# Rotary turn of queries and keys by four row transfers instead of a permutation product

## The chip, the cores and the metric

The kernel runs on one core of a Trainium2 chip. The metric is the device time of one execution in microseconds, lower is better. TensorE is PE in the profile (its weight loads are PEld), VectorE is DVE, ScalarE is ACT, GpSimd is POOL, and SP is the engine whose queue fetches the weights.

## The reference, cut to what matters

Two transformer-like blocks are computed for 256 positions of 2048 values. The first has two layers. In each layer a projection `w_in` (2048 to 6144) gives the input of a state-space mixer, gates, and the queries, keys and values of eight heads of differential attention. The change touches only the rotary turn of those queries and keys:

```python
def apply_rope(t, cos, sin):
    half = HEAD_DIM // 2
    tf = t.astype(jnp.float32)
    t1, t2 = tf[..., :half], tf[..., half:]
    return jnp.concatenate([t1 * cos - t2 * sin, t2 * cos + t1 * sin], axis=-1).astype(t.dtype)

q = apply_rope(q.reshape(bsz, s, ATTN_HEADS, 2, HEAD_DIM), cos, sin)
k = apply_rope(k.reshape(bsz, s, ATTN_HEADS, 2, HEAD_DIM), cos, sin)
```

HEAD_DIM is 64, so within each group of 64 rows the two groups of 32 rows change places, and one of them changes its sign. The second block has an RWKV mixer, a latent attention with a small rotary part of its own (tiles `kpe` and `qp`), and a feed-forward part. All arithmetic is float32 within the tolerance of the reference.

## The kernel before, in words

Everything is kept transposed: a tile is 128 features (partitions) by 256 positions. A projection is a stream of output tiles. Each output tile of `w_in` is the sum of 16 blocks, and each block is three matmuls of rounded float32 values (high weight part with high and low activations, low weight part with high activations). The weights are fetched in halves of 8 blocks (512 KB) on SP's queue; ACT makes the high part of a half (`hi`), DVE the low part (`lo`). Four halves of room (`NS = 4`) are kept, so ACT may make half p as soon as PE has finished half p - 4, and there are three halves between the two.

One list of beats, made by the class `Timeline`, fixes the order of work of all five engines. Each engine plays the beats that concern it in that order, with semaphore waits on what the others do. The list is the matmul blocks of the streams; at the end of an output tile its evacuation `ev` begins, phase 0 with the end of the tile, and one further phase at every eighth block after it. In between, background generators give one step each at every second block (`per=2`; every fourth with `per=4`): the state-space mixer (`s5`, 16 rounds per layer, each a preparation `s5_prep` and a run `s5_run`), the attention of a head (`att`, 15 steps) and, in the second block, the RWKV heads (`rw`, 15 steps each, eight heads, in the stream of `w_in2` from tile 28 on). How many background steps lie behind each step of a generator is written out by hand in the tuples `S5_PREP`, `S5_RUN`, `S5_PHASE`, `S5_START`, `ATTENTION`, `RWKV` and `MOD_REST` (the "rests"). In layer 0 a fourth generator, `modulation`, runs matmuls of the 1 MB units of `w_ada`, which share the weight ring.

The tiles of kind `rope` are the query and the key tile of each head: 2 x 8 heads x 2 layers = 32. Their three phases before the change:

- phase 0, ACT (line 1806): wait for the tile's last matmul, copy it from the accumulator to one of four slots in `TMP`.
- phase 1, PE (line 1112): wait for this copy, multiply it with the signed permutation `rot` (float32, 128 x 128 by 128 x 256) into the second half of the same bank.
- phase 2, DVE (line 2457 on): `o` = turned tile x `SIN`, slot = slot x `COS`, `o` = `o` + slot, `o` being the place of the head's query in `QT` or of its key in `KB`. The attention of the head waits for the last of them (semaphore `ropes`).

A bank of the accumulator is handed on after the first of the three operations of DVE (`BANK_FREE`). `RS` and `RS2` are two rows of 256 columns that hold norm sums and roots at other times. ACT's own queue issues four DMAs, all at the start of the kernel (`begin`).

Of the kernel before, what the change touches and what calls it, by code (L numbers as in the profile page):

```python
# [15 lines left out]
MUL, ADD, SUB, MAX, MIN = ALU.mult, ALU.add, ALU.subtract, ALU.max, ALU.min  # L16
# [31 lines left out]
def const_array():  # L48
    p = np.arange(128)
# [3 lines left out]
    def put(name, a):  # L53
        n = dict(CONSTS)[name]
        c[:, CCOL[name]:CCOL[name] + n] = np.asarray(a, np.float32).reshape(128, -1) if np.ndim(a) else a
# [2 lines left out]
    rot = np.zeros((128, 128))  # L58
    for m in range(128):
        if m % 64 < 32:  # L60
            rot[m + 32, m] = -1
        else:
            rot[m - 32, m] = 1
    put("rot", rot)
# [11 lines left out]
    put("scm", np.broadcast_to(np.arange(256) % 32 != 0, (128, 256)))  # L76
    put("id64", p[:, None] % 64 == np.arange(64)[None, :])
    put("ch4", p[:, None] // 32 == np.arange(4)[None, :])
    put("invf", np.float32(10000.0) ** (-(p % 32).astype(np.float32) / np.float32(32)))
    top = p < 64  # L80
    put("sgn", np.where(top, 1, -1))
    put("ph1", np.where(top, 0.25, 0))
# [43 lines left out]
SIN = _c.alloc(256)  # L126
# [62 lines left out]
class Mem:  # L189
# [26 lines left out]
    def V(self, off, *dims, p0=0, np_=128):  # L216
        t, n, o = (self.ar, N1, off) if off < N1 else (self.up, N2, off - N1)
        return bass.AP(tensor=t, offset=p0 * n + o, ap=[[n, np_]] + self.steps(dims))
# [5 lines left out]
    def B(self, bank, off, *dims, p0=0, np_=128):  # L224
        return bass.AP(tensor=self.ps, offset=p0 * 4096 + bank * 512 + off, ap=[[4096, np_]] + self.steps(dims))
# [22 lines left out]
    def PT(self, k):  # L248
# [8 lines left out]
          "qn": 1, "qp": 3, "kn": 1, "v2": 3, "brw": 1, "bmla": 3, "mo": 2, "up0": 4, "up1": 5, "e": 1, "d0": 1,  # L257
          "d1": 3, "pg": 4}

BANK_FREE = {"u": "ev_act", "z": "ev_dve", "rope": "ev_dve", "v": "ev_act2", "ga": "ev_act", "gb": "ev_act",  # L260
             "xa": "ev_dve", "xo": "ev_dve", "xf": "ev_dve", "rw": "ev_rs", "kpe": "ev_dve", "cq": "ev_rs", "gate": "ev_rs", "qn": "ev_act",
             "qp": "ev_dve", "kn": "ev_act", "v2": "ev_act2", "brw": "ev_dve", "bmla": "ev_dve", "mo": "ev_act",
             "up0": "ev_rs", "up1": "ev_rs", "e": "ev_act", "d0": "ev_act", "d1": "ev_dve", "pg": "ev_act"}
# [11 lines left out]
def kind_of(name, n):  # L275
# [19 lines left out]

QUADS = (("w_in", 48), ("w_pg", 0))

S5_PREP = ((0, 0, 3, 7, 1, 5, 0, 3, 0),
    (0, 2, 0, 4, 2, 6, 2, 2, 0))
S5_RUN = ((1, 3, 1, 7, 1, 3, 1, 2),  # L300
    (1, 5, 2, 6, 1, 3, 1, 1))
S5_PHASE = ((18, 1),
    (17, 2))
S5_START = (6, 8)
ATTENTION = ((1, 1, 3, 2, 3, 4, 4, 1, 2, 1, 1, 2, 5, 2, 1),
    (1, 1, 2, 2, 1, 1, 4, 1, 5, 2, 3, 3, 3, 1, 2))
RWKV = (1, 3, 3, 6, 3, 4, 2, 2, 2, 1, 2, 2, 2, 4, 1)
MOD_REST = (2, 3, 2)


class Tile:
# [634 lines left out]
class Port:  # L946
# [22 lines left out]
    def put(self, ins):  # L969
        self.newest = Op(self, ins)  # L970
        return self.newest
# [118 lines left out]
def tensor_program(pe, m, tl, D):  # L1090
# [18 lines left out]

    def ev(t, ph):  # L1110
        b = t.bank
        if t.kind in ("rope", "qp", "kpe") and ph == 1:
            pe.wait_ge("ev_rs" if t.kind == "kpe" else "ev_act", ("ev", t.o))
            pe.mm(B(b, 256, 256), con("rot"), V(TMP + 256 * t.slots[0][0], 256), True, True).then_inc("ev_pe", ("ev", t.o))
        if t.kind in ("v", "v2") and ph == 1:
            s = TMP + 256 * t.slots[0][0]
            pe.wait_ge("ev_act", ("ev", t.o))
            pe.tr(B(b, 256, 128), V(s, 128))
            pe.tr(B(b, 384, 128), V(s + 128, 128)).then_inc("ev_pe", ("ev", t.o))
# [391 lines left out]
def scalar_program(act, m, tl, D):  # L1511
# [280 lines left out]
    def ev(t, ph):  # L1792
# [13 lines left out]
        elif t.kind in ("rope", "v", "qp", "v2") and ph == 0:  # L1806
            s = tile_ready(act, t.slots[0])
            act.act(V(s, 256), pv, ACT.Copy).then_inc("ev_act", key)
        elif t.kind in ("v", "v2") and ph == 2:
            hd = (n - 8) // 4  # L1810
            if t.kind == "v" and hd >= 2:
# [95 lines left out]
def vector_program(dve, m, tl, D):  # L1907
# [535 lines left out]
    def ev(t, ph):  # L2443
# [10 lines left out]
        if t.kind == "z" and ph == 1:  # L2454
            dve.wait_ge("ev_act", key)
            dve.stt(s, s, 1.0, pv, ADD, MUL).then_inc("ev_dve", key)
        elif t.kind in ("rope", "qp", "kpe") and ph == 2:
            if t.kind == "rope":
                hd = (n - 8) // 4
                o = V(KB + 256 * (hd % 2) if (n - 8) % 4 else QT + 256 * hd, 256)  # L2460
# [2 lines left out]
            else:  # L2463
                o = V(KPE if t.kind == "kpe" else QP + 256 * (n - 8), 256)
            dve.wait_ge("table_act", 1 if t.kind == "rope" else 2)
            dve.wait_ge("ev_pe", key)
            dve.tt(o, B(b, 256, 256), V(SIN, 256), MUL).then_inc("ev_dve", key)
            dve.tt(s, s, V(COS, 256), MUL)
            dve.settle()
            dve.tt(o, o, s, ADD).then_inc("ropes", key)  # L2470
# [460 lines left out]
```

## Time and profile before

| what | us |
|---|---|
| three runs | 2893.70, 2898.98, 2899.66 |
| median | 2898.98 |
| the profiled execution | 2895.5 |
| its span, first to last instruction | 2893.6 |
| PE busy | 2781.8 (96%) |
| DVE busy | 2008.9 (69%) |
| ACT busy | 1468.2 (51%) |
| DMA share of the 16 engines | 54.2% for SP's queue, 5.4% for POOL's |

The granted TensorE clock is 0.985 of 2.4 GHz over the span. Times of stretches are counted from the first instruction. Matched with the list of beats, the stretches are: layer 0's `w_in` from tile 8 on about 168 to 524, the rest of layer 0 to 698, layer 1's `w_in` from tile 8 on about 750 to 1045 (its rope tiles end at 984), RWKV heads 1354 to 1698, the tail of RWKV to 1739. A busy PE is no measure of speed, since matmuls overlap; the start-to-start time of the big matmuls is.

### The profile page before, as it was taken

What the parts mean: (1) busy time and instruction counts of PE and PEld (TensorE: products, weight loads), DVE (VectorE), ACT (ScalarE), POOL (GpSimd) and SP (SyncE); (2) the same over time, 40 slices, a digit from 0 to 9 for tenths busy, and PEclk for the clock granted to TensorE, in tenths of its full rate; (3) what the DMA queues carried; (4) which work ended last, traced back from release to release, by engine and by line L of the source; (5) the groups of instructions that cost most, each with busy time, mean ns of one, the idle gap of its engine ahead of it and who ended that gap; (6) DMA issues with size and microseconds to landing.
All of it is one profiled execution on the core that took longest, in us unless ns stands there. A gap on an engine that the chain in (4) does not pass through costs nothing.

```text
span 2893.6 us, 64415 instructions
## 1 busy us (share of the span) xinstructions
PE 2781.8 (96%) x27664; PEld 2593.9 (90%) x27664; DVE 2008.9 (69%) x3478; ACT 1468.2 (51%) x2406; POOL 288.5 (10%) x488
## 2 busy tenths in 40 slices
PE   6899999999999999999999999999999999999987
PEld 2678788788999999999889889999999999999987
DVE  6357778687799986765556566666888547887565
ACT  3335556355566656644444435456555445555454
POOL 0012222100123221200011011100000000000000
PEclk9899999999999999999999999999999999999999
DMA  9988788885756566555444445554555555555543
GB/s 392 332 267 269 260 287 267 292 310 169 205 171 199 175 204 197 181 175 169 140 144 150 140 133 170 180 193 161 185 182 187 184 184 180 181 185 187 182 153 110
DMA packets 168236, 581.08 MB, mean 201 GB/s; under 512 B 40272, under 2 KB 40304, under 8 KB 155536
## 3 DMA queue, kind: packets, MB, share of 16 engines
q1 hardware_dynamic: 146784, 525.40, 54.2%
q0 software_dynamic: 20592, 48.26, 5.4%
q8 instruction: 218, 3.57, 0.5%
q10 hardware_dynamic: 576, 3.31, 0.3%
q14 instruction: 66, 0.54, 0.1%
HBM read 555.06 MB, written 21.76 MB: 199 GB/s over the span
## 4 chain that ended last, share of the span: by engine, by line
PE 84%; DVE 7%; DMA 6%; ACT 1%; issue 1%; SPq 1%; POOL 0%; DVEq 0%; ACTq 0%
PE acc L1011 82%; DMA arena<-in_w_ada 3%; DVE arena L979 2%; PE acc L1014 2%; DVE rounded L979 2%; DMA scr_k<-arena 1%; DMA arena<-scr_k 1%; SPq L976 1%; DVE upper L987 1%; DMA scr_u<-upper 0%; DVE arena L987 0%; ACT arena L1008 0%; DVE rounded L987 0%; DVE upper L979 0%; DMA arena<-in_w_outm 0%
## 5 line engine op out<-in xcount | busy, mean ns | idle before, releaser
L1011 PE MATMUL acc<-rounded 128*128 128x256 f32 x14592 | 1861.9, 286 | 18.6 <-issue 10.1
L1011 PEld LDWEIGHTS acc<-rounded 128*128 128x128 f32 x14592 | 1783.5, 192 | 86.2 <-issue 61.2
L1008 ACT ACTIVATE rounded<-arena 128x1024 fp32r<-128x1024 f32 (+1 forms) x862 | 875.3, 1022 | 694.5 <-PE acc L1011 583.5
L979 DVE TENSOR_TENSOR rounded<-arena,rounded 128x1024 fp32r<-128x1024 f32 (+1 forms) x830 | 983.9, 1198 | 246.7 <-ACT rounded L1008 246.1
L1011 PEld LDWEIGHTS acc<-upper_rounded,rounded 128*128 128x128 f32 x4656 | 560.8, 192 | 18.2 <-issue 9.8
L1011 PE MATMUL acc<-upper_rounded,rounded 128*128 128x256 f32 x4656 | 567.7, 284 | 2.8 <-DVE rounded L979 2.0
L1008 ACT ACTIVATE arena<-arena 128x256 f32<-128x256 f32 (+3 forms) x473 | 232.9, 515 | 170.8 <-DVE arena L979 105.4
L979 DVE TENSOR_TENSOR arena<-acc,arena 128x256 f32<-128x256 f32 (+5 forms) x270 | 113.7, 431 | 233.7 <-PE acc L1011 221.0
L979 DVE TENSOR_TENSOR arena<-arena 128x256 f32<-128x256 f32 (+5 forms) x455 | 233.3, 526 | 35.9 <-ACT arena L1008 27.5
L987 DVE SCALAR_TENSOR_TENSOR arena<-arena 128x256 f32<-128x256 f32 (+5 forms) x465 | 205.1, 446 | 27.7 <-ACT arena L1008 19.6
L1011 PE MATMUL acc<-arena 128*32 128x512 f32 (+6 forms) x1990 | 183.2, 402 | 41.7 <-DMA arena<-in_w_ada 27.6
L1008 ACT ACTIVATE arena<-acc 128x256 f32<-128x256 f32 (+3 forms) x267 | 99.2, 384 | 187.6 <-PE acc L1011 179.2
L1011 PEld LDWEIGHTS acc<-arena 128*32 128x32 f32 (+2 forms) x1990 | 69.6, 123 | 97.0 <-DMA arena<-in_w_ada 50.7
L1008 ACT ACTIVATE upper<-acc 128x128 f32<-128x128 f32 (+3 forms) x184 | 67.4, 380 | 114.2 <-PE acc L1011 82.5
L1008 ACT ACTIVATE arena<-acc,arena 128x256 f32<-128x256 f32 (+1 forms) x148 | 59.3, 428 | 103.3 <-PE acc L1011 91.2
L1011 PE MATMUL acc<-upper 32*32 32x32 f32 (+8 forms) x4384 | 101.3, 218 | 9.1 <-issue 3.3
L1011 PEld LDWEIGHTS acc<-upper 32*32 32x32 f32 (+4 forms) x4384 | 73.1, 114 | 30.0 <-issue 13.5
L976 POOL DMA_DIRECT2D arena<-scr_k x128 | 77.3, 621 | 122.5 <-DMA scr_k<-arena 121.8
L1011 PE MATMUL acc<-upper,arena 64*64 64x64 f32 (+4 forms) x490 | 63.0, 350 | 13.7 <-DMA upper<-in_w_ada 6.9
L976 POOL DMA_DIRECT2D scr_g<-arena x56 | 30.4, 545 | 440.4 <-DVE arena L990 236.6
L1014 PE MATMUL acc<-arena 128*128 128x128 f32 x416 | 71.2, 276 | 2.8 <-ACT arena L1008 2.3
L1008 ACT ACT_TABLE_LOAD x56 | 71.8, 1283 | 4.0 <-issue 3.0
(92 smaller groups left out, 1116.0 us busy)
## 6 DMA issues: line engine op xcount, KB each, us to landing
arena<-in_w_in SPq DMA_DIRECT2D x328, 512.0 KB, 4.8
arena<-in_w_ada SPq DMA_DIRECT2D x88, 1024.0 KB, 5.5
arena<-in_w_up SPq DMA_DIRECT2D x176, 512.0 KB, 3.9
arena<-in_w_down SPq DMA_DIRECT2D x88, 512.0 KB, 4.2
arena<-in_w_outa SPq DMA_DIRECT2D x32, 512.0 KB, 6.0
arena<-in_w_glu SPq DMA_DIRECT2D x32, 512.0 KB, 5.8
arena<-in_w_outm SPq DMA_DIRECT2D x32, 512.0 KB, 4.6
arena<-in_w_out SPq DMA_DIRECT2D x32, 512.0 KB, 3.8
```

The source lines that it names most:

```text
L976: self.e.dma_start(out, in_).then_inc(self.signals.sems[sem], 16)
L979: return self.put(self.e and self.e.tensor_tensor(o, a, b, op))
L987: return self.put(self.e and self.e.scalar_tensor_tensor(out=o, in0=a, scalar=s, in1=b, op0=o1, op1=o2))
L1008: return self.put(self.e and self.e.activation(o, a, f, scale=scale, **kw))
L1011: return self.put(self.e and self.e.matmul(o, l, r, start=start, stop=stop, skip_group_check=True))
L1014: return self.put(self.e and self.e.transpose(o, i, self.m.con("ident")))
```

## The change

1. The PE instruction of phase 1 is gone for `rope` tiles. `kpe` and `qp` tiles keep it.
2. ACT, after its copy of phase 0, waits until DVE has done with the tile that used the same row four tiles earlier (from tile 12 on), waits for its own copy, and issues four DMAs on its own queue. Each moves 32 rows of 256 values (32 KB) of the slot to the neighbouring group of 32 rows of `RS` (query tiles) or `RS2` (key tiles).
3. DVE's first operation of phase 2 waits for these four DMAs instead of PE, and reads `RS` or `RS2` instead of the accumulator.
4. The sign is moved from `rot` to the table of frequencies, so that `SIN` comes out signed; `COS` is even and stays.
5. The bank is free after ACT's copy.
6. The rests are different.

```diff
-            rot[m + 32, m] = -1
+            rot[m + 32, m] = 1
...
-    put("invf", np.float32(10000.0) ** (-(p % 32).astype(np.float32) / np.float32(32)))
+    put("invf", np.where(p % 64 < 32, -1, 1) * np.float32(10000.0) ** (-(p % 32).astype(np.float32) / np.float32(32)))
...
-BANK_FREE = {"u": "ev_act", "z": "ev_dve", "rope": "ev_dve", "v": "ev_act2", "ga": "ev_act", "gb": "ev_act",
+BANK_FREE = {"u": "ev_act", "z": "ev_dve", "rope": "ev_act", "v": "ev_act2", "ga": "ev_act", "gb": "ev_act",
...
-S5_PREP = ((0, 0, 3, 7, 1, 5, 0, 3, 0),
-    (0, 2, 0, 4, 2, 6, 2, 2, 0))
-S5_RUN = ((1, 3, 1, 7, 1, 3, 1, 2),
+S5_PREP = ((0, 0, 3, 7, 2, 5, 0, 2, 1),
+    (0, 2, 3, 3, 0, 6, 2, 2, 0))
+S5_RUN = ((1, 4, 1, 7, 1, 3, 1, 1),
     (1, 5, 2, 6, 1, 3, 1, 1))
-S5_PHASE = ((18, 1),
-    (17, 2))
-S5_START = (6, 8)
-ATTENTION = ((1, 1, 3, 2, 3, 4, 4, 1, 2, 1, 1, 2, 5, 2, 1),
-    (1, 1, 2, 2, 1, 1, 4, 1, 5, 2, 3, 3, 3, 1, 2))
-RWKV = (1, 3, 3, 6, 3, 4, 2, 2, 2, 1, 2, 2, 2, 4, 1)
-MOD_REST = (2, 3, 2)
+S5_PHASE = ((13, 6),
+    (18, 1))
+S5_START = (5, 8)
+ATTENTION = ((1, 1, 3, 2, 3, 4, 4, 1, 1, 1, 1, 2, 6, 2, 1),
+    (1, 1, 2, 2, 1, 1, 4, 1, 5, 1, 3, 4, 3, 1, 2))
+RWKV = (2, 4, 4, 5, 3, 1, 1, 1, 1, 1, 2, 3, 3, 3, 1)
+MOD_REST = (2, 3, 1)
...
-        if t.kind in ("rope", "qp", "kpe") and ph == 1:
+        if t.kind in ("qp", "kpe") and ph == 1:
...
             act.act(V(s, 256), pv, ACT.Copy).then_inc("ev_act", key)
+            if t.kind == "rope":
+                if n >= 12:
+                    act.wait_ge("ev_dve", ("ev", tl.out_of["w_in", l, n - 4].o))
+                act.wait_ge("ev_act", key)
+                for q in range(4):
+                    act.dma(V((RS, RS2)[n % 4], 256, p0=32 * q, np_=32), V(s, 256, p0=32 * (q ^ 1), np_=32), f"swap{n % 4}", (t.o, q))
...
-            dve.wait_ge("ev_pe", key)
-            dve.tt(o, B(b, 256, 256), V(SIN, 256), MUL).then_inc("ev_dve", key)
+            if t.kind == "rope":
+                dve.wait_ge(f"swap{n % 4}", (t.o, 3))
+                half = V((RS, RS2)[n % 4], 256)
+            else:
+                dve.wait_ge("ev_pe", key)
+                half = B(b, 256, 256)
+            dve.tt(o, half, V(SIN, 256), MUL).then_inc("ev_dve", key)
```

## Rows read from the trace of the kernel before

**Rows 1.** Busy time by stretch; the columns are named in the second line.

```profile
core 0: us, PE busy (x) PEld busy (x) DVE busy (x) ACT busy (x) POOL busy (x), PEclk, DMA share, GB/s
200.00:524.00 324.00, 319.28 (x2838) 263.38 (x2837) 256.41 (x482) 180.18 (x378) 77.33 (x129) 1.00 0.81 271
750.00:984.00 234.00, 232.03 (x2146) 218.43 (x2145) 212.21 (x397) 146.75 (x308) 65.86 (x108) 1.00 0.60 183
1354.00:1698.00 344.00, 332.50 (x6927) 303.98 (x6926) 194.01 (x394) 149.01 (x266) 32.57 (x60) 1.00 0.44 143
1698.00:1739.00 41.00, 36.89 (x612) 34.33 (x611) 27.69 (x51) 11.06 (x16) 7.34 (x11) 0.96 0.35 114
```

**Rows 2.** The chain that ended last, shares of the span by engine.

```profile
PE 84%; DVE 7%; DMA 6%; ACT 1%; issue 1%; SPq 1%; POOL 0%; DVEq 0%; ACTq 0%
```

**Rows 3.** Timeline of PE, layer 1: start, us, instruction, shapes, count.

```profile
753.19 6.00 PE L1011 MATMUL acc<-rounded 128*128 128x256 f32 x48
759.12 0.64 PE L1011 MATMUL acc<-arena,upper 128*32 128x128 f32 x16
...
766.02 1.70 PE L1011 MATMUL acc<-rounded 128*128 128x256 f32 x12
767.56 0.59 PE L1011 MATMUL acc<-arena 128*128 128x256 f32 x2
767.80 3.23 PE L1011 MATMUL acc<-rounded 128*128 128x256 f32 x24
770.87 0.82 PE L1014 MATMUL acc<-arena 128*128 128x128 f32 x6
```

**Rows 4.** Timeline of ACT's queue at the start: its only four DMA issues.

```profile
0.72 0.41 ACTq L976 DMA_DIRECT2D arena<-in_params  x1
...
2.12 0.77 ACTq L976 DMA_DIRECT2D arena<-in_x  x1
```

**Rows 5.** The line of all DMA issues, and issues by tensor (KB, us to landing).

```profile
L976 SPq DMA_DIRECT2D arena<-in_w_in x328: 327/328/1931, 90.5 to 1673.1; - x164
DMA to landing us min/median/max: 2.0/4.4/20.5
...
arena<-scr_k POOLq DMA_DIRECT2D x128, 64.0 KB, 4.8
arena<-in_params ACTq DMA_DIRECT2D x1, 8.0 KB, 5.2
```

**Rows 6.** Timelines of ACT and DVE: three rope tiles, copy and first operation.

```profile
917.25 0.36 ACT L1008 ACTIVATE arena<-acc 128x256 f32<-128x256 f32 x1
917.52 1.05 ACT L1008 ACTIVATE rounded<-arena 128x1024 fp32r<-128x1024 f32 x1
...
920.48 0.42 DVE L979 TENSOR_TENSOR upper<-acc,arena 128x256 f32<-128x256 f32 x1
...
757.07 0.39 ACT L1008 ACTIVATE arena<-acc 128x256 f32<-128x256 f32 x1 [1.27 <-PE acc L1011]
...
761.37 0.42 DVE L979 TENSOR_TENSOR upper<-acc,arena 128x256 f32<-128x256 f32 x1 [1.70 <-PE acc L1011]
...
442.26 0.36 ACT L1008 ACTIVATE arena<-acc 128x256 f32<-128x256 f32 x1
...
453.26 0.42 DVE L979 TENSOR_TENSOR upper<-acc,arena 128x256 f32<-128x256 f32 x1
```

**Rows 7.** Who PE waited for, 200 to 524.

```profile
PE acc L1011 <- DMA arena<-scr_k: 2.6, 2, 1.9
```

**Rows 8.** Timeline of ACT and PE inside RWKV head 3, steps 8 and 9.

```profile
1515.16 0.28 ACT L1008 ACTIVATE upper<-acc 128x128 f32<-128x128 f32 x1 [0.31 <-PE acc L1011]
...
1516.65 0.45 PE L1011 MATMUL acc<-upper 32*32 32x32 f32 x32
```

**Rows 9.** Timeline of PE at the end of RWKV, after the last block of `w_in2`.

```profile
1732.86 4.33 PE L1011 MATMUL acc<-arena,upper 128*64 128x128 f32 x48 [0.77 <-DVE upper L993]
1738.01 1.09 PE L1011 MATMUL acc<-arena,upper 128*64 128x128 f32 x16 [0.83 <-DVE arena L979]
```

More of the change, by code:

```diff
@@ L2456, in ev @@
             dve.stt(s, s, 1.0, pv, ADD, MUL).then_inc("ev_dve", key)
-        elif t.kind in ("rope", "qp", "kpe") and ph == 2:
+        elif t.kind in ("qp", "kpe") and ph == 2 or t.kind == "rope" and ph == 2:
             if t.kind == "rope":
```

## The prediction

> **What bounds the kernel now.** I read four views in this order. The chain that ended last comes first: PE holds 84% of it, DVE 7%, DMA 6% and ACT 1% [rows 2]. Whatever takes matmul time off PE therefore shortens the kernel, as long as no other engine is close behind. The busy times by stretch say who is close behind [rows 1]. In layer 0 (200 to 524) PE is busy 319.3 of 324 us, DVE 256.4, ACT 180.2. In layer 1 (750 to 984) PE is busy 232.0 of 234 us, but DVE 212.2 as well; only 21.8 us of that stretch is free on DVE. ACT has 146.7 of 234. So layer 0 is PE's alone, while in layer 1 DVE stands some 9% behind PE. Then the timeline of PE gives the price of one permutation product, and the timelines of ACT and DVE side by side give the time that a transfer may take. The clock is 1.00 of 2.4 GHz in both stretches, so it has nothing to give.
>
> **The product that goes.** The cost of a product is the PE time that it inserts between big matmuls. Without anything between them 48 big matmuls take 759.12 - 753.19 = 5.93 us, 0.1235 us each. From 766.02 to 770.87 there are 36 big ones and one product: 4.85 us, less 36 x 0.1235 = 4.45, leaves 0.40 us [rows 3]. The same arithmetic one product earlier, over 24 big ones, gives 0.45. I take 0.42. There are 32 of them, 16 in each layer: 32 x 0.42 = 13.4 us, between 12.8 and 14.4. The product's second record (0.59 us for the pair) overlaps the next matmuls, so 32 x 0.59 would count too much. The weight load goes with it.
>
> **What ACT gets.** Four DMA issues for each rope tile. ACT's queue issued four DMAs in the whole kernel before, in 0.41 to 0.77 us each [rows 4]; on SP one issue takes 0.33 us [rows 5]. I take 0.45, with 0.33 and 0.77 as bounds: 1.8 us for a tile (1.3 to 3.1), 58 us in all (42 to 99). In layer 1 that makes 146.7 + 16 x 1.8 = 175.5 of 234 us, so ACT doesn't become the bound. Queued behind it is nearly always the high part of a weight half: `hi` starts 0.27 us after the copy began [rows 6]. By the code it has until three halves later, 3 x 24 x 0.1235 = 8.9 us, so a delay of 1.8 us does not reach PE that way. It reaches DVE, which makes the low part from it and takes other beats only in order. The wait for the tile four back is over long before (four tiles are 24 us and more), and the wait for its own copy ends with it. I count this part at 0 for PE in layer 0 and put it in the DVE term for layer 1. Without the cover it would be 1.8 us a tile.
>
> **When the swapped rows arrive.** No row shows a transfer from SBUF to SBUF, so I bound it. From issue to landing all DMAs take 2.0 us at least and 4.4 in the median; the smallest one on ACT's queue took 5.2, and the nearest in size, 64 KB, 4.8 [rows 5]. The last of four issues starts 3 x 0.45 = 1.35 us after the copy. Thus the rows are there 1.35 + 4.4 = 5.7 us after the copy, with bounds 3 x 0.33 + 2.0 = 3.0 and 3 x 0.77 + 5.2 = 7.5. DVE's first operation began 2.87 us after the copy's end in the tightest tile (920.48 against 917.61), 3.9 us in another one, where it waited for the product itself, and 10.6 us in one of the loosest [rows 6]. The three stand for 32 tiles; read in the same way for all, the median is 6.9 us, 7 of the 32 are under 5.2 and 12 under 5.9. Adding up what is missing to 5.7 us gives about 4 us of DVE waiting in layer 0 and 7 in layer 1; missing to 3.0 it is 0.1 in all, missing to 7.5 about 15 and 21. The three DVE operations themselves keep their size: 0.42 us from the accumulator, 0.41 from SBUF [rows 6]. In layer 0 DVE has 68 us free [rows 1] and the wait is hidden.
>
> **A rule that speaks against it.** The trace has transfers to landing in 2.0 to 5.2 us at these sizes [rows 5]. The Trainium skill, "DMA: Bandwidth & Descriptors", section "Rules for kernel authors", says that transfers under 64 KB pay mostly overhead, and that transfers to disjoint partition groups serialize, so one for all partitions is better. If the four came one after another by the page's fixed 2 us, the rows would be there about 8 us after the copy, an estimate from that page. Rows can't decide it, and it is the slower rival below, priced from rows.
>
> **What it comes to in layer 1.** PE would need 6.7 us less there, so DVE's 21.8 us of free time shrink to 15.1. Of these, from the count of DVE's operations, some 5 us are gaps under 0.2 us between dependent operations that don't compress. The remaining 10 must hold the 7 us of waiting for rows and whatever ACT's delay adds (16 tiles at up to 1.8 us, mostly hidden by beats in between; I take 3). That is just enough; PE begins to feel single late low parts. I take 2 us lost, between 0 and 7 (the whole gain of this layer).
>
> **The bank** that is free earlier brings nothing: it is used again three tiles later, after DVE's operation in every tile I looked at, and PE names no wait for it. The signed table costs no instruction.
>
> **The rests.** RWKV: the tuple sums to 38 steps before and 35 after, of two blocks each. Eight heads end 8 x 3 x 2 = 48 blocks earlier, 48 x 3 x 0.1235 = 17.8 us of matmuls, so the closing steps that now run alone after the last block fall into the stream. PE's free time in that tail is 41 - 36.9 = 4.1 us, two pieces of it 0.77 and 0.83 [rows 1, 9]; the rest of it is PE work that stays. I take 2 us gained, 0 to 4. Against it, the rests behind steps 5 to 8 fall to 1, that is by 0.74 us a step in three of four. PE came 1.21 us after ACT's copy in such a step (1516.65 against 1515.44) [rows 8], so 0.47 us is left; a `hi` of 1.05 us in front of that copy would turn it into a stall. I take 1.5 us lost, 0 to 8. In layer 0 the run's step 4 moves one step away from the load of the taps, for which PE waited 2.6 us [rows 7]: 1.5 us gained, 0 to 3. The other rests shift single steps by 0.7 us and sum to the same; 0, plus or minus 2. `MOD_REST` moves eight units earlier by one step each, once 0.9 us at most. Sum of the rests: -2, from -9 to +12.
>
> **Sum.** -13.4 + 2 - 2 = -13.4 us. Against the profiled execution, 2895.5 us, that is 2882; the median of the three runs is 3.5 us above it, and against this median it is 2885.6. I predict 2886.
>
> **Rivals.**
> 1. The rows come late and DVE becomes the bound in layer 1. Point from which it decides: rows later than about 7 us after the copy. At 9.5 us, four landings behind each other at 2.0 to 2.4 us, 14 of 16 tiles wait and the missing time sums to about 45 us; less the 10 us of compressible free time and less the lead of the low parts, about 5 us once, PE loses 30 us and gains 6.7, while layer 0 still gains 6.7 and hides its 36 us. Net +16, 2915. For it: the only ACT issue of a small transfer took 5.2 us. Against: that one flew beside 2 MB of others, and the DMA share is 0.60 in layer 1.
> 2. The gain is real in layer 0 only. ACT's 1.8 us and the rows' waits together take up DVE's free time: 6.7 us of layer 1 gone, the shortened RWKV rests cost 3 more instead of bringing anything: -13.4 + 6.7 + 1 = -5.7, 2893. For it: DVE at 212 of 234.
> 3. The rests are worth more than I can count from sums: stalls in front of the mixer's steps and in RWKV go as well, 8 us more: 2877.
> 4. The change doesn't shorten PE, because the stream is paced by weight fetches. In layer 0 the DMA share is 0.81 [rows 1]. Then 2899. Against: PE names 2.6 us of DMA waits in 324 us [rows 7].
>
> **How the numbers follow.** Forecast (2879 to 2892) 0.57; rival 3 (under 2879) 0.11; rival 2 (2892 to 2900) 0.15; rival 4 (2896 to 2902) 0.04; rival 1 (over 2902) 0.13. A measurement of this kernel can tell about 0.2%, 5.8 us, so faster means under 2893.2. It has the forecast, rival 3 and a quarter of rival 2: 0.72. Slower means over 2904.8: rival 1 but for its mild end, 0.12. Same: 0.16. The range leaves out most of rival 1 and the end of rival 3: 2874 to 2904.
>
> **What would show it.** Right: no product records in the stretches of `w_in`; the stretch from 200 to 984 shorter by some 12 us; the first DVE operation of a rope tile named as waiting for the transfer in about a third of tiles, up to 3 us. Wrong: issues on ACT above 0.8 us; landing after more than 7 us; DVE free time near nothing in layer 1 with PE waiting for `rounded` from DVE; more than 5 us of new PE waits between 1354 and 1698. The forecast also fails if the new rests cost something in the mixer's rounds that their sums don't show.

## The result, and the profile after

The changed kernel takes 2916.94 us (median of 6 runs, 2912.99 to 2927.02), the kernel before 2898.27. The ratio is 1.0066, with a 95% interval from 1.0048 to 1.0084: slower by 19 us, where 2886 was forecast. The profiled execution of after spans 2914.5 us.

The rows of after that answer to [rows 1] are these (the same stretches of time, which hold less work once the kernel is behind; the columns are the same). PE's busy time falls by 3.3 us in layer 0 and by 14 us in layer 1. Neither is a saving: in layer 0 PE is idle for 8.1 of 324 us, where it was for 4.7, and in layer 1 for 16 of 234 us, where it was for 2.

```profile
200.00:524.00 324.00, 315.94 (x2799) 261.45 (x2799) 256.92 (x482) 180.04 (x376) 75.69 (x129) 0.99 0.83 278
750.00:984.00 234.00, 217.97 (x1983) 203.62 (x1982) 200.28 (x372) 136.50 (x289) 62.19 (x101) 0.99 0.58 180
```

The chain that ended last, shares by engine (before: [rows 2]). PE has lost 5 points of it; ACT, ACT's queue and "issue" have gained 5 together, DVE one.

```profile
PE 79%; DVE 8%; DMA 6%; ACT 3%; issue 2%; ACTq 2%; SPq 0%; POOL 0%; DVEq 0%
```

The new issues, from the line of all DMA issues of after (duration of one in ns: least, median, most; before: [rows 4, 5]):

```profile
L976 ACTq DMA_DIRECT2D arena<-arena x128: 513/613/1750, 178.6 to 989.2; - x128
```

Their row in the list of issues by tensor (KB, median us to landing):

```profile
arena<-arena ACTq DMA_DIRECT2D x128, 32.0 KB, 4.1
```

One issue takes 0.61 us in the median and up to 1.75, against the 0.45 that I took. A single transfer lands as quickly as I took it, 4.1 us after its issue. All four of a tile are there 6.4 us after the copy's end in the median and 9.3 us at most, where I had 5.7 with 7.5 as the upper bound.

To see where the 19 us come from I cut the kernel into stages, at PE's first product of a stage's output tile. Three stages matter: `w_in` of layer 0 and of layer 1, each from tile 8, where the rope tiles are, and RWKV's part, from the first block that carries it to the first product of `q_up`. The table has all runs of this study. "Nothing" is the time in RWKV's part for which PE stood and the profile names no releaser ("issue" in the rows). The ratio is that of the whole kernel to runs of before made beside it (their medians lie from 2896.7 to 2899.7 us), with its interval.

| run | layer 0 | layer 1 | RWKV | "nothing" | median us, ratio |
|---|---|---|---|---|---|
| before | 355.7 | 295.3 | 386.9 | 4.4 | 2898.27 |
| e11_before_again | 355.3 | 295.3 | 392.6 | 6.4 | one run |
| after | 354.8 | 311.8 | 394.3 | 9.5 | 2916.94, 1.0066 (1.0048 to 1.0084) |
| e1_old_rests | 358.0 | 308.7 | 397.0 | 11.0 | 2925.53, 1.0088 (1.0075 to 1.0102) |
| e3_no_swap | 350.2 | 293.5 | 396.6 | 9.9 | 2899.57, 0.9996 (0.9986 to 1.0006) |
| e12_no_swap_again | 351.1 | 293.3 | 399.0 | 9.0 | one run |
| e4_issue_no_wait | 362.3 | 304.3 | 394.5 | 9.7 | 2923.51, 1.0085 (1.0071 to 1.0099) |
| e10_two_issues | 356.0 | 296.6 | 392.4 | 5.9 | 2905.74, 1.0027 (1.0013 to 1.0041) |
| e5_sp_issue | 356.1 | 300.3 | 395.5 | 8.1 | 2909.0, 1.0037 (1.0024 to 1.0050) |
| e9_pool_issue | 353.9 | 305.4 | 393.7 | 8.6 | 2912.35, 1.0048 (1.0032 to 1.0064) |
| e7_dummy_product | 347.7 | 294.0 | 389.4 | 4.9 | 2894.45, 0.9985 (0.9976 to 0.9995) |
| e2_new_rests | 351.2 | 296.1 | 406.5 | 15.8 | 2908.52, 1.0039 (1.0023 to 1.0054) |
| e6_rwkv_rests | 351.7 | 295.3 | 411.4 | 21.1 | 2911.58, 1.0047 (1.0033 to 1.0061) |
| e8_early_rests | 355.2 | 296.0 | 396.6 | 6.9 | 2898.35, 0.9999 (0.9987 to 1.0012) |
| e13_pad_half | 349.9 | 295.4 | 394.4 | 8.2 | 2901.12, 1.0011 (1.0001 to 1.0020) |
| e16_pad_full | 354.1 | 295.3 | 393.7 | 6.3 | 2897.41, 1.0003 (0.9990 to 1.0016) |
| e14_new_rests_pad | 353.0 | 296.1 | 397.2 | 11.3 | 2905.55, 1.0020 (1.0007 to 1.0032) |
| e15_rwkv_rests_pad | 352.3 | 295.3 | 396.9 | 12.4 | 2902.49, 1.0016 (1.0007 to 1.0026) |

Before it is read, one thing about its grain. Layer 1 repeats to 0.2 us from one profile to the next. RWKV's part doesn't: before itself shows 386.9 and 392.6, and e8, whose instructions there are the same, 396.6. Layer 0 lies between 349.9 and 355.7 in kernels with the same mechanism there. So layer 1 can be read to a few tenths, the other two only by several profiles or by the ratios.

The same stage in whole, before and after, then who PE waited for in it (us in total, times, longest) and whom DVE waited for most:

```profile
750.00:1045.40 295.40, 292.66 (x2711) 276.40 (x2710) 270.05 (x504) 187.23 (x389) 83.48 (x137) 1.00 0.59 183
```

```profile
747.20:1059.00 311.80, 292.65 (x2678) 274.17 (x2677) 271.32 (x505) 186.81 (x389) 82.62 (x137) 0.99 0.57 180
```

PE's waits there, before:

```profile
PE acc L1011 <- DVE upper L979: 1.5, 2, 1.0
PE acc L1014 <- ACT arena L1008: 0.8, 1, 0.8
```

and after:

```profile
PE acc L1014 <- ACT arena L1008: 8.1, 10, 1.8
PE acc L1014 <- DVE arena L987: 5.6, 4, 3.1
PE acc L1011 <- ACT upper L1008: 2.4, 2, 1.9
```

DVE's waits in the same stage, after:

```profile
DVE rounded L979 <- ACT rounded L1008: 18.6, 13, 4.5
DVE upper L979 <- DMA arena<-arena: 4.1, 4, 2.7
```

The wait for the new rows themselves is small (4.1 us, on DVE, and 5.2 in layer 0). What has grown are waits for ACT: PE's from 0.8 to 8.1 us, and DVE's for `rounded` from 3.9 to 18.6. In layer 0 the same line of PE's waits grows from 1.5 us,

```profile
PE acc L1014 <- ACT arena L1008: 1.5, 1, 1.5
```

to 7.2:

```profile
PE acc L1014 <- ACT arena L1008: 7.2, 6, 1.8
```

One place shows how. The timeline of ACT, PE and DVE of after:

```profile
828.45 0.36 ACT L1008 ACTIVATE arena<-acc 128x256 f32<-128x256 f32 x1
...
828.89 3.58 ACTq L976 DMA_DIRECT2D arena<-arena  x4
...
832.52 1.06 ACT L1008 ACTIVATE rounded<-arena 128x1024 fp32r<-128x1024 f32 x1 [3.71 <-issue]
833.48 0.36 ACT L1008 ACTIVATE arena<-acc 128x256 f32<-128x256 f32 x1
833.61 1.23 DVE L979 TENSOR_TENSOR rounded<-arena,rounded 128x1024 fp32r<-128x1024 f32 x1 [0.55 <-ACT rounded L1008]
...
833.90 0.44 PE L1014 MATMUL acc<-arena 128*128 128x128 f32 x2 [1.82 <-ACT arena L1008]
```

The rope tile is copied at 828.45. ACT then issues four transfers, for 3.58 us, and runs nothing meanwhile. Behind them stand a `hi` and, behind that, a copy of the mixer's run (`xt`, out of the accumulator). PE makes its two transposes from this copy, and stands still 1.82 us for it. By the shapes and the number of transposes, 5.8 of the 8.1 us of such waits in layer 1 are for copies of the mixer, the rest for copies of the attention.

### The profile page after: what moved, and what is told of

The parts are those of the page before. It is cut to its first block, busy times and chain, and to the rows that moved or that the text cites. A ratio compares the mean times of both kernels' runs of the same rounds, so it can differ in the third digit from the quotient of the medians.

```text
span 2914.5 us, 64420 instructions
## 1 busy us (share of the span) xinstructions
PE 2780.6 (95%) x27600; PEld 2591.2 (89%) x27600; DVE 2009.3 (69%) x3478; ACT 1467.0 (50%) x2406; POOL 286.7 (10%) x488
## 4 chain that ended last, share of the span: by engine, by line
PE 79%; DVE 8%; DMA 6%; ACT 3%; issue 2%; ACTq 2%; SPq 0%; POOL 0%; DVEq 0%
PE acc L1011 78%; DMA arena<-in_w_ada 3%; DVE arena L979 3%; DVE rounded L979 2%; ACTq L976 2%; ACT arena L1008 1%; PE acc L1014 1%; ACT rounded L1008 1%; DMA upper<-in_w_ada 1%; DVE arena L987 1%; DVE upper L987 1%; ACT L1008 1%; DVE upper L979 0%; DVE rounded L987 0%; DMA scr_k<-arena 0%
## 5 line engine op out<-in xcount | busy, mean ns | idle before, releaser
L1011 PE MATMUL acc<-arena 128*32 128x512 f32 (+7 forms) x1926 | 166.6, 404 | 37.9 <-DMA arena<-in_w_ada 24.5
L1011 PEld LDWEIGHTS acc<-arena 128*32 128x32 f32 (+2 forms) x1926 | 61.5, 122 | 88.8 <-DMA arena<-in_w_ada 46.0
L1014 PEld LDWEIGHTS acc<-arena 128*128 128x128 f32 x416 | 48.1, 141 | 30.2 <-ACT arena L1008 19.1
```

What stands on the lines that cost most here:

```text
L1011: return self.put(self.e and self.e.matmul(o, l, r, start=start, stop=stop, skip_group_check=True))
L1014: return self.put(self.e and self.e.transpose(o, i, self.m.con("ident")))
```

## Experiments

The theory after the comparison: ACT's four issues delay its own copies, and that is the loss. The rival: DVE waits for the rows' landing. A second question is why RWKV's part is longer, in which the mechanism changes nothing.

The runs e3, e4, e5, e7, e9, e10 and e12 are made from the changed kernel with before's rests; its signed table and its earlier bank stay.

**e1_old_rests.** The change with the tuples of rests of before: the mechanism alone.

```
-RWKV = (2, 4, 4, 5, 3, 1, 1, 1, 1, 1, 2, 3, 3, 3, 1)
+RWKV = (1, 3, 3, 6, 3, 4, 2, 2, 2, 1, 2, 2, 2, 4, 1)
...   and S5_PREP, S5_RUN, S5_PHASE, S5_START, ATTENTION, MOD_REST likewise
```

> The changed kernel with all rests of the kernel before. Theory A: the four issues on ACT (0.61 us each in the changed kernel, 2.5 us a tile) hold up the small ACT steps of the mixer and of the attention that PE waits for, and the new rests cost only in RWKV, where PE took 394.2 us instead of 386.8. Then this one gives some 2909, with layer 1's w_in from tile 8 on near 310 us and RWKV near 387. Theory B: the loss is all in the new rests, the transfers do what they should. Then 2885, with layer 1 near 289.

Measured: 2925.53 us, ratio 1.0088, above both expectations. The mechanism alone costs 25 us. Layer 1 is at 308.7 us, where theory A had it, but RWKV's part takes 397.0 us with the old rests too, so the new rests are not what lengthens it. They give 6 us back (1.0088 to 1.0066), which is about the uncertainty of that difference.

**e2_new_rests.** Before with the new tuples, that is with those lines the other way round: the rests alone.

> The kernel before with the new rests alone, the product stays on PE. Theory A: RWKV 7 us longer, the rest within 3: 2905. Theory B: all of the loss plus the missing gain: 2917 + 13 = 2930, with layer 1 above 310 us.

Measured: 2908.52 us, 1.0039. With the product in place the same rests cost 11 us. What they bring seems to be no fixed amount; e6 and e8 take this up.

**e3_no_swap.** No product and no transfer: DVE multiplies the slot itself by the sines (the turned half of the rope is left out).

```
-        if t.kind in ("rope", "qp", "kpe") and ph == 1:
+        if t.kind in ("qp", "kpe") and ph == 1:
...
-            dve.wait_ge("ev_pe", key)      # for rope tiles alone
-            dve.tt(o, B(b, 256, 256), V(SIN, 256), MUL)
+            dve.wait_ge("ev_act", key)
+            dve.tt(o, s, V(SIN, 256), MUL)
```

> Old rests, no product and no transfers: DVE multiplies the slot itself by the sines, so the turned half is left out of the computation. This is what the change could gain at most: 32 x 0.42 = 13.4 us, 2885. If DVE is the bound of layer 1, as the prediction feared, the 6.7 us of that layer come out smaller than those of layer 0: 2890 or more.

Measured: 2899.57 us, 0.9996. Without any cost of the swap, taking the products away brings nothing that can be told. Layer 1 shows why, first the stage in whole:

```profile
745.00:1038.50 293.50, 286.71 (x2679) 271.09 (x2677) 270.06 (x503) 186.83 (x389) 83.94 (x137) 1.00 0.60 183
```

and whom PE waited for in it:

```profile
PE acc L1014 <- DVE arena L987: 2.3, 4, 1.0
PE acc L1011 <- DVE upper L979: 2.0, 2, 1.0
PE acc L1014 <- ACT arena L1008: 1.9, 3, 0.8
```

PE is busy 286.7 us instead of 292.7, 6 us less, 0.37 a product. But the stage is only 1.9 us shorter: PE's free time has grown from 2.7 to 6.8 us, in front of operations of DVE and ACT, which are as busy as before (270.1 and 186.8). In layer 0 PE's busy time falls by 6.9 us. The stage is shorter by some 3.5: the three profiles without the old product or a transfer (e3, e12, e7) have 349.7 us in the mean, the six with the product and the same early rests (before, e11, e6, e13, e15, e16) 353.2, and the two groups overlap. And RWKV's part is 4 to 12 us longer than in the two profiles of before, with not one instruction changed in it. So the total of this run is a small gain and a loss elsewhere that has nothing to do with the swap.

**e4_issue_no_wait.** e3, and ACT issues four transfers of the same size for each rope tile, out of the table of cosines; the results are not used, and DVE waits only once in a layer, at the last step of attention, for the last of them (the turned half is left out).

```
+            if t.kind == "rope":
+                act.wait_ge("table_act", 1)
+                if n >= 12:
+                    act.wait_ge(f"swap{n % 4}", (tl.out_of["w_in", l, n - 4].o, 3))
+                act.wait_ge("ev_act", key)
+                for q in range(4):
+                    act.dma(V((RS, RS2)[n % 4], 256, p0=32 * q, np_=32),
+                            V(COS, 256, p0=32 * (q ^ 1), np_=32), f"swap{n % 4}", (t.o, q))
...
+            if h == 7:              # DVE, attention, step 14
+                for part in range(2):
+                    dve.wait_ge(f"swap{part}", (tl.out_of["w_in", l, 36 + part].o, 3))
```

> As e3_no_swap, and ACT issues its four transfers (from the cosine table into the rows, so the turned half is left out of the computation), but nobody waits for their landing at once. Theory A, the issues cost: the same as e1_old_rests within 3 us. Theory C, the landing costs (DVE waits and the low parts come late): near e3_no_swap, 2885 to 2890.

Measured: 2923.51 us, 1.0085; e3 has 0.9996 beside the same runs of before. Issuing alone costs 26 us (12 in layer 0 and 11 in layer 1 by the table), and with the wait for the landing (e1) the ratio is 1.0088. So the landing adds 1 us, give or take 6, and the rival falls as the main cause. PE's waits in layer 1, without any landing to wait for:

```profile
PE acc L1014 <- ACT arena L1008: 6.8, 10, 1.3
PE acc L1014 <- DVE arena L987: 5.0, 4, 2.6
PE acc L1011 <- ACT upper L1008: 2.2, 2, 1.8
```

These are nearly the waits of after; in layer 0 the wait for ACT's copies is 12.8 us.

**e10_two_issues.** e4 with two issues.

```
-                for q in range(4):
+                for q in range(2):
```

> As the run in which ACT issues four transfers that nobody waits for, with two issues a tile instead of four (the turned half of the rope stays left out). If each issue delays ACT's next copies by its own length and PE feels all of it: layer 1's w_in about 299 us, half way between 293.5 (none) and 304.3 (four), and 2911 us in all. If there is slack to be used up first: 295 us and 2902 in all.

Measured: 2905.74 us, 1.0027, between the two expectations. Layer 1 takes 293.5, 296.6 and 304.3 us with none, two and four issues: the first two cost 3 us there, the second two 8. Two issues (1.14 us, at 572 ns each) mostly fit into what the copies of layer 1 had in hand; the next two don't. In layer 0 the steps are more alike (350.2 or 351.1, 356.0 and 362.3 us). The whole kernel loses 9 us with the first two and 17 with the second. PE's waits, the same lines:

```profile
PE acc L1014 <- ACT arena L1008: 2.9, 4, 1.3
PE acc L1014 <- DVE arena L987: 2.5, 3, 1.3
```

**e5_sp_issue.** e1, with the issues on SP's queue.

```
+    def ev(t, ph):          # in sync_program; the same lines are gone from scalar_program
+        if t.kind == "rope" and ph == 0:
+            n, l, s = t.n, t.l, TMP + 256 * t.slots[0][0]
+            if n >= 12:
+                sp.wait_ge("ev_dve", ("ev", tl.out_of["w_in", l, n - 4].o))
+            sp.wait_ge("ev_act", ("ev", t.o))
+            for q in range(4):
+                sp.dma(...)
```

> The changed kernel with the rests of before, its four row transfers issued by SP instead of ACT; everything else, the wait of DVE for the landing included, stays. Theory (what costs is that ACT's own copies queue behind four issues of 0.6 us): layer 1's w_in (mm 1152 to 1920) back to about 351 us as in the run without transfers, from 364 to 368, and 2900 us in all (2896 to 2904). Rival (the rows come too late, DVE waits): 2920 or more, since the landing is the same or later on SP's queue, which also issues the weights. The stretch of RWKV should be 381 us as in the other runs without products, whoever issues.

Measured: 2909.0 us, 1.0037, between what the two expected. Moving the issues off ACT takes away 15 of the 25 us, most of it, not all. The same transfers still fly, so it is not their traffic that costs: PE's waits for ACT's copies in layer 1, 10.4 us in e1, are 2.4 us. What shows in layer 1 now is that DVE waits for the rows. DVE's longest waits there:

```profile
DVE upper L979 <- DMA arena<-arena: 9.2, 2, 5.9
```

and PE's:

```profile
PE acc L1014 <- DVE arena L987: 4.7, 3, 3.6
PE acc L1011 <- DVE upper L979: 3.4, 3, 1.4
```

Two waits only, but one of 5.9 us. The transfers themselves land sooner than on ACT's queue (3.2 us after issue in the median). It is the issue that comes late, as the timeline of this wait shows:

```profile
755.97 5.24 SPq L976 DMA_DIRECT2D upper<-scr_u  x6
756.45 0.38 ACT L1008 ACTIVATE arena<-acc 128x256 f32<-128x256 f32 x1 [1.27 <-PE acc L1011]
...
761.26 2.41 SPq L976 DMA_DIRECT2D arena<-arena  x4
...
764.95 0.42 DVE L979 TENSOR_TENSOR upper<-arena 128x256 f32<-128x256 f32 x1 [5.91 <-DMA arena<-arena]
```

The copy ends at 756.83. SP is in the middle of six other issues and comes to these four at 761.26, 4.4 us later. In most tiles it comes within 0.1 us.

**e9_pool_issue.** The same on POOL's queue.

```
+        elif t.kind == "rope" and ph == 0:     # in gpsimd_program
+            if n >= 12:
+                pool.wait_ge("ev_dve", ("ev", tl.out_of["w_in", l, n - 4].o))
+            pool.wait_ge("ev_act", key)
+            for q in range(4):
+                pool.dma(...)
```

> The changed kernel with the rests of before, its four row transfers issued by POOL instead of ACT. POOL has little work beside w_in, but its issues may take longer and wait for its own stores. Theory (issues cost only what is queued behind them): layer 1's w_in as with SP or better, 296 to 301 us of 308.7 with ACT, and about 2905 us in all (2899 to 2910). Rival (the last 9 us that SP's version keeps above the run without transfers are the landing, which DVE waits for): no better than SP's, 2909 or more.

Measured: 2912.35 us, 1.0048. An issue takes 0.51 us there, but DVE waits 12.7 us in layer 1 for the rows (5 times, 4.6 at most), and the stage takes 305.4 us. POOL's program waits in order for the landing of other transfers (123 us in 31 waits for `scr_k` in the whole run), and its first issue comes 0.3 us after the copy in the median but 8.5 us in the worst tile. The rival of this run holds: no queue of the three carries the swap for free.

**e6_rwkv_rests and e8_early_rests.** Before with RWKV's new tuple alone (the line below), and with all the other new tuples but that one.

```
-RWKV = (1, 3, 3, 6, 3, 4, 2, 2, 2, 1, 2, 2, 2, 4, 1)
+RWKV = (2, 4, 4, 5, 3, 1, 1, 1, 1, 1, 2, 3, 3, 3, 1)
```

> Before with only the tuple of RWKV's rests changed. The run with all new rests had its RWKV part, tail included, 20 us longer and the stages ahead of it 10 us shorter. If RWKV's rests do this by themselves: 2917 us (2913 to 2921), stream 405 us, tail 1.5. If the 20 us came from somewhere else (what the earlier rests moved): 2899.

> Before with all new rests but RWKV's. The stages ahead of RWKV were some 10 us shorter with the new rests and before's mechanism; PE's instructions are as many, so RWKV should stay at 372 us and its tail at 14.6: 2889 us (2886 to 2893). Rival (the stages' gain was bought by work pushed into RWKV, whose stream then takes longer whatever its own rests): 2899 or more.

Measured: 2911.58 (1.0047, less than the 2913 to 2921 expected) and 2898.35 (0.9999). RWKV's tuple alone is the loss of e2. It does take away the tail as forecast: the closing steps after the last block went from 14.6 us to 1.5. But the stream before it grew by 37.6 us, from 372.3 to 409.9. The closing steps moved into it are 13.1 of these. The waits that have no releaser grew by 16.7; before, and e6:

```profile
PE acc L1011 <- issue: 4.4, 6, 1.4
```

```profile
PE acc L1011 <- issue: 21.1, 16, 2.5
```

The rest, some 8 us, goes with PE's clock, granted at 0.97 over the part where before has 1.00.

The early rests were worth nothing that can be told; e8 lies nearer to its rival than to the 2889 expected. RWKV begins 8.5 us earlier in e2 than in before; in e8 it is 2.7 us, and 4.5 of the 8.5 are layer 0, within its scatter.

**e7_dummy_product.** e3, and in place of each product one of 16 columns between constants (the turned half is left out).

```
+        if t.kind == "rope" and ph == 1:
+            pe.wait_ge("ev_act", ("ev", t.o))
+            pe.mm(B(b, 256, 16), con("rot"), con("rot", 16), True, True)
```

> As the run without transfers and products (the turned half of the rope left out), but a product of 16 columns between constants takes the place of each of the 32 products, so that PE's instructions are as many as in before and lie where they lay. Theory (the 8.7 us that RWKV's stream loses without the products come from the places at which PE's instructions are fetched, against its bursts of short matmuls): RWKV's stream back to 372 us (371 to 375), PE's waits for nothing there from 9.9 us back to about 4.4, and 2892 us in all (2889 to 2896). Rival (the loss comes from data, clock or DVE): stream 381 and 2900 us.

Measured: 2894.45 us, 0.9985 (0.9976 to 0.9995), the fastest run of the study, as its theory had it. PE's waits for nothing in RWKV fell from 9.9 to 4.9 us, and the part from 396.6 to 389.4, although no instruction of RWKV differs between the two. One profile of a part that scatters by 10 us does not show this by itself. The program of e7 is 32 entries shorter than before's and 117 longer than e3's, as they are counted below.

**e11_before_again and e12_no_swap_again.** The same kernels once more.

No line differs.

> Before once more, for a second profile of it. If the 8 to 9 us by which RWKV's stream is longer in the other runs (380 to 381 against 372.3 us, with the same instructions) belong to their layout, this one shows 372 to 374 again, with the same waits for nothing at the same steps and no fall of the clock between 1360 and 1720. If they are chance (where a fetch of instructions takes longer, and whether the clock then falls for 3.4 or 6.8 us), it may show anything from 372 to 381, and waits at other lengths.

> The run without transfers and products once more, for a second profile (the turned half left out). Layout: RWKV's stream 381 us again, with PE's wait for nothing of 2.5 us at the same step and the clock's fall behind it. Chance: a stream somewhere between 372 and 381, and the waits at other lengths.

Measured: the stream takes 378.0 us (372.3 the first time) and 383.2 (381.0). Both halves of the expectation are right in part. The waits keep their places and change their lengths. I numbered PE's matmuls and weight loads from the end of the program. Places with a wait for nothing and over 0.6 us between two starts fall in RWKV only at certain numbers: 32643, 29331, 27552 and 22203 in before, 30860, 29331, 27552, 23732 and 22203 in its repeat; 32749, 29183, 25876, 25366, 24092, 21800 and 20527 in e3, and in its repeat, e1 and e5 numbers of this list with 27404 and, in e1, 22309 besides. Neighbours differ by multiples of 254 to 255 (29331 - 27552 = 7 x 254.1).

This count leaves out PE's semaphore instructions, which stand in its program too: 545 in before, four instructions of other kinds among them. Counted with them, from the program's start, the step is 256. In the 18 profiles of this study PE has 112 waits for nothing over 0.6 us in RWKV's part, and every one of them stands 193 or 194 entries behind a multiple of 256. The page has a queue that fits, packets and MB of before:

```profile
q8 instruction: 218, 3.57, 0.5%
```

PE's 27,664 matmuls, as many weight loads and the 545 others are 55,873 entries, 218.3 times 256, and one packet has 16.4 KB, 64 bytes for each of 256 entries. The changed kernel has 55,724 entries, 217.7 times 256, and 217 packets.

**e13_pad_half and e16_pad_full.** Before with 32, or 64, small products at PE's start, while it waits for its first weights: 128, or 256, more entries.

```
+        if first and not pads:
+            pads.append(0)
+            for i in range(32):     # 64 in the other
+                pe.mm(B(3, 256, 16, np_=32), V(CA, (0, 32)), V(CA, 16), True, True)
```

> Before with 32 products of 16 columns between constants at PE's start, while it waits for weights (128 more entries in PE's program, nothing else). In the traces so far PE's waits for nothing in RWKV fall only at certain entries of its program, some 255 apart (at the entries 29331 and 23732 before the end with the products, at 29183, 25876 and 24092 without them). Layout: 128 entries shift this grid by a half, to about where it lies without the products, so RWKV's stream takes 377 to 383 us instead of 372 to 378 and waits for nothing 8 to 11 us instead of 4.4 to 6.4; 2901 us in all. Rival (the waits belong to chance or to the data): 4.4 to 6.9 us, at before's entries.

> As the first of this call, with 64 such products, 256 entries. Layout: the grid is back where before has it: stream 372 to 378 us, waits for nothing 4.4 to 6.4 us at before's entries (29331, 23732 or 22203 before the end), 2898 us in all. If the padding itself did something else to the stretch, it would be more here than with half of it.

Measured: 2901.12 (1.0011, from 1.0001 to 1.0020) and 2897.41 (1.0003). With half a step the waits stand at 32770, 29204, 27425, 24113, 21821 and 20547, each some 21 from a number of e3 or its repeat, and sum to 8.2 us; with a whole step they stand at 29331, 27552 and 22203, before's, and sum to 6.3. The packets follow, with 219 for the whole step (56,129 entries). It is the places that show the cut; the times alone would not, since the streams (379.4 and 377.8 us) lie beside the 378.0 of before's repeat. One burst of 96 short matmuls shows it in all four: before, its repeat, a whole step, half a step.

```profile
1465.01 0.86 PE L1011 MATMUL acc<-upper 32*32 32x32 f32 x74
1467.22 0.38 PE L1011 MATMUL acc<-upper 32*32 32x32 f32 x22 [1.35 <-issue]
```

```profile
1465.64 0.86 PE L1011 MATMUL acc<-upper 32*32 32x32 f32 x74
1468.69 0.54 PE L1011 MATMUL acc<-upper 32*32 32x32 f32 x22 [2.19 <-issue]
```

```profile
1465.69 0.86 PE L1011 MATMUL acc<-upper 32*32 32x32 f32 x74
1469.80 0.53 PE L1011 MATMUL acc<-upper 32*32 32x32 f32 x22 [3.25 <-issue]
```

```profile
1464.09 0.45 PE L1011 MATMUL acc<-upper 32*32 32x32 f32 x30
1466.13 0.50 PE L1011 MATMUL acc<-upper 32*32 32x32 f32 x34 [1.59 <-issue]
```

The first three are cut after 74 of them, the fourth elsewhere. The place belongs to the program, the length (1.35, 2.19 and 3.25 us) to the run. That these are PE's instructions arriving late, packet by packet, is inferred from the step of 256, from the count and size of the packets, and from the places moving with the padding; no row names the releaser.

A long wait costs more than itself. The stretch behind the 3.25 us, with the granted clock in the third column from the end:

```profile
1469.00:1475.80 6.80, 6.00 (x106) 5.65 (x106) 0.29 (x1) 0.56 (x2) 0.00 (x0) 0.52 0.03 12
```

0.52 is nearly all at the lower of PE's two levels, 1.2 GHz. The next 12 big matmuls take 2.93 us there; behind the 1.35 us wait of before, where the clock stays at 1.00, they take 1.69. Behind the waits of 2.19 us (the repeat) and 1.59 us (half a step) they take 2.90 and 2.59.

**e14_new_rests_pad and e15_rwkv_rests_pad.** e2 and e6 with the same 32 small products.

> The run with all new rests and before's products, with the same 128 entries more at PE's start. Layout: its grid comes to lie where it lies in the changed kernel, whose RWKV part took 394 us with 9.5 us of waits for nothing, against 406.5 us and 15.8 without the padding; so about 394 to 397 us there and 2897 us in all (2893 to 2902), from 2908.5. Rival: 406 us and 2908 again.

> Before with RWKV's new rests alone and the same 128 entries more. Layout: RWKV's part, 411 us with 21.1 us of waits for nothing without the padding, goes to 394 to 399 us; 2899 us in all (2894 to 2904), from 2911.6. Rival: 411 us and 2911 again.

Measured: 2905.55 (1.0020, was 1.0039) and 2902.49 (1.0016, was 1.0047). RWKV's part goes from 406.5 to 397.2 and from 411.4 to 396.9 us, as the layout asks, and the waits for nothing from 15.8 to 11.3 and from 21.1 to 12.4. In e14 the total follows only in part (by the ratios 5.5 us, for 9 in RWKV) and misses its expectation of 2893 to 2902.

All profiles but e7's together, by tuple and cut: with before's cut and the old tuple RWKV's part has 386.9, 392.6, 396.6 (e8) and 393.7 us (e16), with the new tuple 406.5 and 411.4. With the cut of the changed kernel or half a step (these two lie 21 entries apart) the old tuple has from 392.4 to 399.0 in eight profiles, the new one 394.3, 396.9 and 397.2. So the new tuple costs 16 to 17 us with before's cut and about 1 with the other, which can't be told from nothing. The cut itself moves the old tuple's part by some 3 us in the mean, inside its scatter of 10, and the new tuple's by 13, beyond it.

No run that computes the whole reference beat before.

## Why the prediction was wrong

The ratios in a row, each less the one before it, times 2898 us: taking the products away -1.2 (e3), four issues on ACT's queue +25.8 (e4), waiting for the landing +0.9 (e1), the rests -6.4 (after); together +19.1. The first has 3 us of uncertainty, the others, being differences, 5 to 7. So only the issues stand clear of it.

**What gave way.** The step that failed is in "What ACT gets": that behind the issues there is "nearly always the high part of a weight half", with 8.9 us of lead, and that the delay reaches DVE only, "0 for PE in layer 0". Behind some of them stand ACT's copies for the mixer and the attention, which PE takes with the next step of their generator, not three halves later: its waits for them go from 0.8 to 8.1 us in layer 1, and in layer 0 from 1.5 to 7.2. I had read three tiles [rows 6], and the one whose successor I looked at had a `hi` behind it. The sentence "without the cover it would be 1.8 us a tile" had the size right: 32 tiles by 1.8 is 58 us, at 0.61 us an issue 78, of which 26 reached the end.

**The issue's price.** I took 0.45 us from two rows of the start [rows 4] and one of SP [rows 5], and named 0.77 as the upper end. Measured 0.61 in the median, but up to 1.75, and 3.58 us for four in the place shown. The bound was no bound.

**The rows' landing.** Forecast were 4.4 us from issue to landing, 5.7 us from the copy to the last row, and 4 us of DVE waiting in layer 0 and 7 in layer 1. Measured were 4.1, 6.4 (up to 9.3), and 5.2 and 4.1 us of waiting, in 10 of 32 tiles and 2.7 us at most. This was right, though 12 of 32 tiles came later than the 7 us that I had written down as a sign of being wrong. With it rival 1 fell as a mechanism. The result lies at its 2915 all the same, from another cause; that this number fits is luck.

The rule of the Trainium skill that I had set against it ("DMA: Bandwidth & Descriptors", "Rules for kernel authors", on two halves of the partitions) would have had the last row there about 8 us after the copy, an estimate from the page's 2 us. The trace has 6.4 us in the median (7.5 in layer 0, 6.3 in layer 1), between my 5.7 and that 8, so these runs don't decide the rule.

The same page of the Trainium skill ("Anatomy of one DMA", on the path of GpSimd) puts some 50 ns on the sequencer's dispatch of a DMA and calls the making of its descriptors small. On that path e9 shows 507 ns of POOL in the median for one of these transfers, ten times as much.

On the other two queues, of which that section doesn't speak, the rows show 613 ns on ACT's and 591 on SP's for these transfers and 328 for SP's weights [rows 5]. Here this is what decides.

**The product.** 0.42 us each, 13.4 in all. PE's busy time fell by 6.9 and 6.0 us in e3, 12.8 together, 0.40 each: the size was right. What the stages gave was about 3.5 and 1.9, and over the whole kernel nothing that can be told, since RWKV's part came out longer. For layer 1 I had 2 us lost of 6.7; it was 4.8 of them, before any swap was paid for. "DVE stands some 9% behind PE" [rows 1] was the view to read more pessimistically: in e3 PE's free time grew in front of single operations of DVE and ACT, so what DVE had free between its operations did not serve PE.

**The rests.** RWKV's tail: 2 us gained of 4.1, measured 13 (14.6 to 1.5), since the closing steps' matmuls moved into the stream. The stream paid it back: the closing steps run there, and the waits for nothing are longer and more. I looked for this price in ACT's copies [rows 8], 0 to 8 us; it was in front of PE's own instructions, a wait that the trace of before had shown (4.4 us of "issue" in RWKV) and that I hadn't read. The sum of the rests, -2 from -9 to +12, holds both -6 (after) and +11 (e2), but by its width and not by its terms: no term of it is the cut of PE's program.

**The rivals.** 4, paced by weights: no, PE's waits for DMA stayed at a few us. 2, only layer 0 gains: its picture was the nearest for e3, but its time left the issues out. The loss that came, copies for PE queued behind issues, was none of them; I had the sentence for it and priced it at nothing. The check I wrote down, "issues on ACT above 0.8 us", would not have caught it either.

## What to carry over

A DMA issue on a computing engine's queue is work of that engine: price it by its rows (here 0.6 us each, four to a tile), and list everything that follows it on that engine with who waits for each, not only what follows in two or three places. And before counting matmul time as time gained, see how busy the engine is that feeds them: here, with DVE at 91% in layer 1, 1.9 of 6.0 us came back.

## What the runs showed of the hardware

- Four transfers of 32 KB within SBUF, issued one behind the other, land 4.1 us after their issue in the median on ACT's queue, 3.2 on SP's (e5) and 3.9 on POOL's (e9). An issue holds its engine 0.61 us on ACT's queue, 0.59 on SP's for the same transfers (0.33 for SP's weights, [rows 5]) and 0.51 on POOL's.
- In RWKV's part PE stands still, with no releaser, for up to 3.3 us at some of the places that lie 256 entries apart in its program, most of it in front of bursts of short matmuls (3.3 of the 4.4 us of before, 9.1 of the 9.9 of e3). All 112 such waits over 0.6 us, in 18 profiles, are at these places.
- The same instructions with the same cut take 386.9 to 396.6 us there, through the lengths of these waits and the clock behind them. Shifting the program by half of that step moves the part with the new rests from 411.4 to 396.9. A difference of under 10 us between two kernels with such bursts is therefore no proof about their algorithm until several profiles, or a version padded to the same cut, have been read.
- Behind the longest of these waits (3.25 us) PE's granted clock was 0.52 over the stretch shown, nearly all of it at 1.2 GHz; behind the one of 1.35 us it stayed at 1.00.
